# Two fused transformer blocks: the first norm's statistics of tokens 128 to 255 are divided between VectorE and ScalarE, the factor of tokens 0 to 127 is made between the two, and the root table's load moves ahead of some small loads

## The reference

```python
def rmsnorm(x, g):
    y = x32 * lax.rsqrt(jnp.mean(x32 * x32, axis=-1, keepdims=True) + NORM_EPS)
    return (y * g).astype(x.dtype)

# first block
u = rmsnorm(h, norm1_g)
proj = u @ w_in                       # 2048 -> 16896 columns
ya = hgrn2_branch(hq, hf, hi, hg, ...) @ w_proj_a
yb = dilated_attention_branch(aq, ak, av) @ w_proj_b
h = h + (sigmoid(gate_a) * ya + sigmoid(gate_b) * yb) @ w_out
h = h + conv_ffn(rmsnorm(h, norm2_g), ...)
x = rmsnorm(h, norm_f_g)
# second block
h = h + concat([recurrent_group(...), spatial_gating_group(...)]) @ w_out_2
h = h + peer(rms_norm(h, ffn_norm_g), ...)   # 128 rows of peer_u and peer_v gathered per token
out = rms_norm(h, final_norm_g)
```

## Time and profile before

| | us |
|---|---|
| median of 3 runs | 3424.25 |
| lowest, highest | 3423.61, 3425.0 |
| profiled execution's own time | 3421.45 |
| its span, first to last instruction | 3419.7 |

### The profile page before, as it was taken

The page is one execution under the profiler, slowest core; times in us unless marked ns, Lnnn a source line. Parts: engine busy times, 40 slices in busy tenths (PEclk is TensorE's granted clock), DMA queues, the critical chain, the costliest instruction groups (busy, mean ns, idle before and its releaser), DMA issues.

```text
span 3419.7 us, 35000 instructions
## 1 busy us (share of the span) xinstructions
PE 3123.8 (91%) x13582; PEld 2276.6 (67%) x13582; DVE 2243.5 (66%) x3450; ACT 1258.8 (37%) x1846; POOL 556.9 (16%) x533
## 2 busy tenths in 40 slices
PE   8999999999999999999999999999777777777776
PEld 6998998888888888888888888843332222222222
DVE  7786777775567787776557776888754454444445
ACT  5554566554445555554446752211110010000001
POOL 0000000000000000000000001653443343333333
PEclk9999999999999999999999999999999999999999
DMA  7555555556555555555556568999999999999998
GB/s 231 161 149 159 157 176 172 173 161 209 185 184 185 185 185 186 184 192 194 200 190 206 182 230 284 413 417 420 420 420 420 420 420 420 421 420 420 420 420 354
DMA packets 405598, 935.89 MB, mean 274 GB/s; under 512 B 16472, under 2 KB 246521, under 8 KB 339129
## 3 DMA queue, kind: packets, MB, share of 16 engines
q0 software_dynamic: 75936, 547.39, 38.8%
q1 hardware_dynamic: 328482, 385.92, 35.1%
q10 hardware_dynamic: 1016, 0.35, 0.0%
HBM read 931.50 MB, written 2.10 MB: 273 GB/s over the span
## 4 chain that ended last, share of the span: by engine, by line
PE 65%; DMA 27%; DVE 5%; issue 1%; ACT 1%; POOL 0%; POOLq 0%; DVEq 0%; SPq 0%; ACTq 0%
DMA Ub<-in_peer_u,ids 26%; PE W L1524 14%; PE W L1532 11%; PE W L1534 11%; PE W L1533 11%; PE W L1522 7%; DVE Ub L2643 4%; PE W L1458 3%; PE M L1585 1%; PE M L1683 1%; PE T L1683 1%; PE W L1521 1%; DMA Vb<-in_peer_v,ids 1%; POOL Vb L2782 0%; PE T L1419 0%
## 5 line engine op out<-in xcount | busy, mean ns | idle before, releaser
L2209 DVE TENSOR_TENSOR wl<-raw,wh 128x1024 fp32r<-128x1024 f32 (+1 forms) x720 | 850.6, 1186 | 563.3 <-ACT wh L1774 561.4
L1774 ACT ACTIVATE wh<-raw 128x1024 fp32r<-128x1024 f32 (+1 forms) x720 | 740.7, 1032 | 892.8 <-PE W L1534 572.6
L2643 DVE CUSTOM_DVE_ANT_0 Ub<-Ub,xn 128x2048 f32<-128x2048 f32 x256 | 585.8, 2291 | 496.6 <-DMA Ub<-in_peer_u,ids 496.5
L1524 PE MATMUL W<-u,wh 128*128 128x512 f32 x2040 | 722.5, 397 | 0.0
L1683 PE MATMUL W<-Vb,diag 128*128 128x512 f32 x996 | 460.5, 605 | 165.3 <-DMA Vb<-in_peer_v,ids 162.8
L1522 PE MATMUL W<-u,wl 128*128 128x256 f32 x2176 | 603.1, 282 | 0.2 <-DVE u L2171 0.2
L1683 PEld LDWEIGHTS W<-Vb,diag 128*128 128x128 f32 x996 | 180.1, 191 | 445.7 <-issue 381.9
L1524 PEld LDWEIGHTS W<-u,wh 128*128 128x128 f32 x2040 | 383.3, 188 | 88.3
L1532 PE MATMUL W<-wh,u 128*128 128x512 f32 (+1 forms) x1152 | 436.1, 379 | 1.2 <-DVE u L2569 1.0
L1534 PE MATMUL W<-wh,u 128*128 128x512 f32 (+1 forms) x1152 | 427.9, 371 | 0.0
L1533 PE MATMUL W<-wl,u 128*128 128x512 f32 (+1 forms) x1152 | 427.6, 371 | 0.0
(11 more groups left out here) (366 smaller groups left out, 3260.1 us busy)
## 6 DMA issues: line engine op xcount, KB each, us to landing
raw<-in_w_in SPq DMA_DIRECT2D x128, 1024.0 KB, 5.3
raw<-in_w_up SPq DMA_DIRECT2D x88, 1024.0 KB, 5.1
raw<-in_w_down SPq DMA_DIRECT2D x44, 1024.0 KB, 5.0
raw<-in_w_in SPq DMA_DIRECT2D x144, 256.0 KB, 3.7
raw<-in_w_out SPq DMA_DIRECT2D x32, 1024.0 KB, 5.0
raw<-in_w_proj_a SPq DMA_DIRECT2D x16, 1024.0 KB, 5.0
Wb<-in_peer_w_q SPq DMA_DIRECT2D x16, 1024.0 KB, 8.4
raw<-in_w_proj_b SPq DMA_DIRECT2D x4, 1024.0 KB, 5.1
```

The costliest lines, as they stand in the source:

```text
L1524: i = q.matmul(o, vh, u[:, :, kk, :], start=False, stop=last)
L1774: q.activation(wh[:, s % NS, 0:b.half], r, ACT.Copy).then_inc(s_hi, 1)
L2209: q.tensor_tensor(wl[:, s % NS, 0:b.half], r, wh[:, s % NS, 0:b.half].bitcast(F32), SUB).then_inc(s_lo, 1)
L2643: q.tensor_tensor_reduce(U[:, :], U[:, :], xn[:, t, :], 1.0, 0.0, MUL, ADD, dots[t][:, k:k + 1]).then_inc(s_dot, 1)
```

## The change

The diff in full:

```diff
--- before.py
+++ after.py
@@ -1064,6 +1064,7 @@
         rstd = low("rstd", [2])
         st6b = low("st6b", [2, 4, 6])
         ms2 = low("ms2", [2])
+        sqsum = low("sqsum", [1])
         rf = low("rf", [2])
         rr = low("rr", [2])
         nsp = low("nsp", [16])
@@ -1230,6 +1231,7 @@
         s_set, s_kept, s_turned, s_lbt, s_lb = sem("set"), sem("kept"), sem("turned"), sem("lbt"), sem("lb")
         s_sp0, s_sp1, s_nsp = sem("sp_min"), sem("sp_exp"), sem("nsp")
         s_ms, s_root, s_rstd, s_xsa, s_xsd = sem("ms"), sem("root"), sem("rstd"), sem("xs_act"), sem("xs_dve")
+        s_later = sem("later_squares")
         s_uT, s_rope, s_ropeT = sem("uT"), sem("rope"), sem("ropeT")
         s_score, s_smax, s_pexp, s_prob, s_probT, s_pv = (sem(f"attn_{n}") for n in ("score", "max", "exp", "prob", "probT", "pv"))
         s_rel, s_rexp, s_kq, s_level, s_cross = (sem(f"scan_{n}") for n in ("rel", "exp", "kq", "level", "cross"))
@@ -1711,6 +1713,8 @@
                 for r0, nm in ((0, "norm1_g"), (16, "norm2_g"), (32, "hg_lb_param"), (64, "hg_norm_g")):
                     src = io[nm].rearrange("o (k p) -> (o k) p", p=P)
                     q.dma_start(st1[r0:r0 + src.shape[0], :], src).then_inc(s_st1, 16)
+                e.wait_ge(s_set, 2)
+                q.preload_act_table(ACT.Sqrt)
                 for r0, src in ((0, io["mix_norm_g_2"]), (16, io["ffn_norm_g_2"]), (32, io["conv_w_2"][0]),
                                 (64, io["conv_b_2"]), (72, None), (80, io["lru_b_a_2"][0]),
                                 (96, io["lru_b_x_2"][0]), (112, io["lru_lambda_2"][0])):
@@ -1719,8 +1723,6 @@
                 q.dma_start(cws[0:88, 0:3, :], io["conv_w"][0].rearrange("o (k p) -> k o p", p=P)).then_inc(s_cws, 16)
                 q.dma_start(cws[0:88, 3, :], io["conv_b"][0].rearrange("(k p) -> k p", p=P)).then_inc(s_cws, 16)
                 q.dma_start(iota[:, :], cslice("iota")).then_inc(s_iota, 16)
-                e.wait_ge(s_set, 2)
-                q.preload_act_table(ACT.Sqrt)
 
             def root(r, src):
                 e.wait_ge(s_ms, r + 1)
@@ -1733,9 +1735,12 @@
 
             def scale():
                 root(0, ms)
-                root(1, ms)
+                e.wait_ge(s_x[1], 16)
+                q.activation(xs[:, 1, 1024:2048], X[:, 1, 1024:2048], ACT.Square, scale=2048 ** -0.5, accum_out=sqsum[:, 0:1]).then_inc(s_later, 1)
                 e.wait_ge(s_rstd, 1)
                 for j in range(4):
+                    if j == 1:
+                        root(1, ms)
                     q.activation(xs[:, 0, CK[j]], X[:, 0, CK[j]], ACT.Copy, scale=rstd[:, 0:1]).then_inc(s_xsa, 1)
 
             def turn(ep, k):
@@ -2113,10 +2118,14 @@
                 q.reciprocal(rstd[:, t:t + 1], sq[:, t:t + 1]).then_inc(s_rstd, 1)
 
             def stats_x():
-                for t in range(2):
-                    e.wait_ge(s_x[t], 16)
-                    for j in range(4):
-                        stats(t, j, X[:, t, CK[j]])
+                e.wait_ge(s_x[0], 16)
+                for j in range(4):
+                    stats(0, j, X[:, 0, CK[j]])
+                mean_square(0)
+                inverse(0)
+                e.wait_ge(s_x[1], 16)
+                for j in range(2):
+                    stats(1, j, X[:, 1, CK[j]])
 
             def turn_g1():
                 e.wait_ge(s_turned, 1)
@@ -2137,10 +2146,14 @@
                 q.tensor_copy(rbs[0][:, :, :], strided(rstd[:, :], [1, 2], [0, P])).then_inc(s_rb, 1)
 
             def scale():
-                for t in range(2):
-                    mean_square(t)
-                for t in range(2):
-                    inverse(t)
+                e.wait_ge(s_dve, me.n)
+                q.bn_aggr(mv[:, 1, :], st6[:, 1, 0:2, :].rearrange("p a b -> p (a b)")).then_inc(s_dve, me.up())
+                e.wait_ge(s_dve, me.n)
+                q.scalar_tensor_tensor(ms[:, 1:2], mv[:, 1, 0:1], mv[:, 1, 0:1], mv[:, 1, 1:2], MUL, ADD).then_inc(s_dve, me.up())
+                e.wait_ge(s_dve, me.n)
+                e.wait_ge(s_later, 1)
+                q.scalar_tensor_tensor(ms[:, 1:2], ms[:, 1:2], 0.5, sqsum[:, 0:1], MUL, ADD).then_inc(s_ms, 1)
+                inverse(1)
                 e.wait_ge(s_rstd, 2)
                 for j in range(4):
                     q.tensor_scalar(xs[:, 1, CK[j]], X[:, 1, CK[j]], rstd[:, 1:2], None, MUL).then_inc(s_xsd, 1)
```

## The result

| | before | changed |
|---|---|---|
| median of 4 runs, us | 3424.3 | 3402.57 |
| lowest to highest | 3423.61 to 3425.0 | 3400.38 to 3403.62 |
| ratio, 95% interval | | 0.9936, 0.9924 to 0.9949 |
| profiled execution, us | 3421.45 | 3403.62 |
| its span | 3419.7 | 3401.7 |

The change makes the kernel 21.7 us faster, 0.64%. The forecast was 3422.6, 1.7 faster, with a range of 3420.0 to 3425.4. The rival called D (addresses, faster) had been given 0.06.

What follows compares the result with a forecast made beforehand. It took the head's chain of waits, then a PE-set middle and gathers at 420 GB/s as bounds. ScalarE 1.98 earlier less a 0.32 wait gave -1.66: 3424.25 - 1.7 = 3422.6, range 3420.0 to 3425.4.

Steps and rivals of the forecast that it cites:

- D: Gathers of expert rows: buffers moved by 32 bytes raise the rate 1%, 11 us faster, 3411.5; chance 0.06.
- E: Gathers of expert rows: buffers moved by 32 bytes lower the rate 1%, 11 us slower, 3435; chance 0.04.
- C: ScalarE's head: square not in the root's table set, extra table loads, 0.3 slower, 3424.6; chance 0.04.
- The head: Work before the first weight matmul: PE starts there at 19.7 instead of 21.39, gaining 1.66 us.
- square and read ready: ScalarE's new square with sum and accumulator read, done at 11.2, before VectorE needs it at 11.85.
- second transpose: PE's first transpose of the second tokens, at 13.15 instead of 14.66, 1.51 earlier.
- first conversion: ScalarE's first weight conversion, after its PSUM copies, starting at 17.33, 1.66 earlier.
- the combining operation: New VectorE operation after the second mean square, 11.85 to 12.07; takes 0.22, adds 0.25 with its gap.
- the aggregate of two parts: VectorE's aggregate after the second half's two statistics, expected to end about 11.57.
- A: ScalarE's queue stands still during the table load among small loads; gain only 1.05, 3423.2; chance 0.15.
- B: Earlier start lost: first weight chunk lands late or PE meets a later unmoved wait; 3424.2; chance 0.08.
- the fourth bank: PSUM bank of transposes, full at 16.61 instead of 18.12; ScalarE comes at 16.29 and waits 0.32.

Runs made afterwards that it cites:

- the pad alone: Kernel before with one unused 32-byte tile where the change puts sqsum, giving buffers behind it the changed kernel's addresses; 3403.35 us against 3422.71, ratio 0.9943.
- e9_end_only: Kernel before with only the upper end of memory moved to a multiple of 256, moving `Vb10` and `Vb11` onto one; 3420.78 us, ratio 0.9994.
- the delay: Kernel before plus the unused 32-byte tile and eight extra one-piece statistics on VectorE ahead of the first aggregate; 3409.24 us, ratio 0.996.
- e2b_head_only: Changed kernel with the sum of squares put in unused values of mv, so no tile moves from the old addresses; 3422.35 us against 3422.78, ratio 0.9998.

## Why the prediction was wrong, by its own steps

**The step that failed is the weighing of D and E.** The mechanism was named with its place (the gathers), its address arithmetic (224 past a multiple of 256 to exactly one) and its point of decision, 0.6% of the rate. The rate moved by 1.6% (378.22 to 384.30 MB in the 900 us from 2400). The sum had the stretch of the gathers at no change, and the cases in which it changes had 0.06 and 0.04. What went wrong is this argument of the text: the slices hold so steady that the rate seems set by something else. A steady rate is what any fixed set of addresses gives: fifteen of the sixteen row buffers started at 224, `Ub1` at 192, and none on a boundary. A trace in which a factor hardly varies says next to nothing on that factor. The 1% "each way", taken from the spread of slices, bounded how one alignment varies and not what another costs. The runs put in its place: 7 GB/s of 420, 19.4 us by the pad alone (3422.71 to 3403.35), of which its profile has 18.2 between the first and the last gather of the first table (2111.2 to 3356.4, 1245.2 against 1263.4).

In time for a row: one of 16 engines moves 8192 bytes in 8192 x 16 / 420 = 312.1 ns before and 307.0 after, 5.1 less on the mean of all rows; the packets' own durations fell by 5.5.

The Trainium skill ("DMA: Bandwidth & Descriptors", How a descriptor splits into AXI transactions) describes the split for the bytes that are fetched. Here the side that moved is the one written, and it gains from the boundary as well. By the page's beats, an estimate, 7 of 263 or 2.7% would go at 224 and 1 of 257 or 0.4% at 32; the runs have 1.6% and 1.3% (378.22 and 379.26 against 384.30 MB). The wasted beats don't fit. An additional transaction, the same for each start, fits the step better, but not the fifth of the rows that start at 224 in the changed kernel and take no longer there. What the cost consists of stays open.

**The range** left D outside by giving it 0.06. It was the one case whose price was many times that of all the others and for which a reason stood in the text; even a range down to its own 3411.5 would have missed 3402.6, since the price was mis-sized too (11 for 19.4). Two sums of the text don't come out, and neither decides anything. E's 3435 is more than 11 above 3422.6. And 1.3 below the forecast and 1 to 1.3 above C give a range of 3421.3 to 3425.6 or 3425.9, not 3420.0 to 3425.4.

**The head was right,** step by step, apart from tenths:

| step | forecast | measured |
|---|---|---|
| first root starts | 9.38 | 9.16 |
| statistics of the second half start | 9.99 | 9.76 |
| square and read ready | 11.2 | 10.92 |
| second root starts | 12.10 | 11.78 |
| second transpose | 13.15 | 12.84 |
| first conversion | 17.33 | 17.07 |
| first weight matmul | 19.7 | 19.44 |
| first gather | 1.7 earlier | 1.8 earlier |

The times differ by about what x landed sooner, 0.23, and by the combining operation, which took 0.16 and not 0.22, and the aggregate of two parts, 0.20 and not 0.26.

**A** is refuted by the load at 3.80 beside the issue at 3.83. **B** is refuted at the new addresses by the delay, which arrives whole; at the old ones e2b_head_only leaves it open. **C** is refuted by the absent second load. The first weight chunk and the fourth bank come to ScalarE together, as worked out: the chunk landed 15.2 after its issue, at 16.9, and the conversion began at 17.07, behind the copies of the fourth bank.

## What to carry to other kernels

Before costing an edit, list what it moves in memory: a 4-byte tile placed low shifted nearly every large buffer, and here that was worth ten times the edit itself. Where gathers run at the transfer limit as here, try their buffers on multiples of 256 bytes; work out the start of each buffer, since one shift need not serve them all. Give each experiment of a small edit a twin in which the addresses stay as they were. A steady rate over a long stretch shows a limit, not that the limit is independent of a setting that never varied.

## What the runs showed of the hardware

Gathers of 8 KB rows ran at 427 GB/s with 19 of 24 rows written to a start on a multiple of 256 bytes, at 421 to 422 with the common start 32, 64, 128 or 192 past one, and at 420 with 224. A packet of 8 KB took 309.2 ns on the mean in the first case, and 313.6 to 314.7 in the others. Two buffers on a boundary among fourteen off it had 310.3 and 310.5 (e9_end_only); three off it among thirteen on it lost nothing (309.0 to 309.6). In the stretch that PE sets, where transfers run far below that (186 GB/s between 1000 and 1500), the same shift of addresses had no visible effect: with the pad alone the first gather is issued at 2111.2, and before at 2111.3. ScalarE's queue issued transfers while the engine loaded a table (load at 3.80 for 1.28, next issue at 3.83).
